# Weight matrices of a hybrid decoder step on one core: each load's bytes stored as one block, a partition's part in one piece

## What is computed

```python
h = rmsnorm(x, norm1_w)
proj = h @ w_in                       # 2048 x 8208: 8 gdn heads (q k v z), 16 gate columns, 8 hgrn heads (q f i z)
...                                   # causal conv, gated delta rule, HGRN2, gated head norms
x = x + mix @ w_out                   # 2048 x 2048
u = relu(rmsnorm(x, norm2_w) @ w_up)  # 2048 x 8192
x = x + (u * u) @ w_down              # 8192 x 2048
y = rmsnorm(x, final_norm_w)
```

## Time and profile before

| what | before |
|---|---|
| median of 3 runs (lowest, highest) | 2914.0 us (2912.57, 2924.3) |
| the profiled execution | 2909.2 us |
| its span, first to last instruction | 2907.5 us |
| TensorE, matmuls | 2869.8 us busy, 99% of the span |
| VectorE, ScalarE, GpSimd | 2056.6, 1137.7, 314.4 us busy |
| mean granted TensorE clock | 0.996 of full speed |
| traffic | 396.61 MB in 516,481 packets, mean 136 GB/s |

### The profile page before, as it was taken

How to read it: one execution, slowest core, us unless ns; L and a number is a source line. 1 busy time by engine, 2 the same in 40 slices (tenths; PEclk the granted TensorE clock), 3 DMA queues, 4 the chain that set the end, 5 groups by cost and what they waited for, 6 DMA issues and landing times.

```text
span 2907.5 us, 53032 instructions
## 1 busy us (share of the span) xinstructions
PE 2869.8 (99%) x22264; PEld 2802.5 (96%) x22264; DVE 2056.6 (71%) x2921; ACT 1137.7 (39%) x1432; POOL 314.4 (11%) x464
## 2 busy tenths in 40 slices
PE   9999999999999999999999999999999999999998
PEld 8999999899999999999999999999999999999998
DVE  6666666656575757665687777777778878888885
ACT  4333333333333333333444444444434444444454
POOL 6201111110101010102100000000000000000111
PEclk9999999999999999999999999999999999999999
DMA  7343647643434344444345544554586666666665
GB/s 211 70 92 73 93 72 79 81 93 74 86 79 87 80 79 80 122 130 139 90 140 156 157 136 146 154 154 136 151 255 205 193 204 192 188 193 203 191 193 199
DMA packets 516481, 396.61 MB, mean 136 GB/s; under 512 B 18930, under 2 KB 484196, under 8 KB 516244
## 3 DMA queue, kind: packets, MB, share of 16 engines
q1 hardware_dynamic: 462272, 267.95, 39.8%
q0 software_dynamic: 22672, 88.35, 8.3%
q10 hardware_dynamic: 31300, 36.93, 4.0%
HBM read 308.80 MB, written 84.37 MB: 135 GB/s over the span
## 4 chain that ended last, share of the span: by engine, by line
PE 84%; DVE 8%; ACT 3%; issue 2%; DMA 1%; ACTq 0%; DVEq 0%; POOL 0%; POOLq 0%
PE main L1369 40%; PE main L1003 26%; PE mx L1369 7%; PE mx L1252 2%; DVE w_lo L1969 1%; PE mx L1075 1%; PE mx L1151 1%; PE mx L1162 1%; PE main L1352 1%; DMA tmp<-rows_scratch 1%; DVE tmp L2090 1%; PE mx L1134 1%; PE mx L1091 1%; DMA mix_scratch<-tmp 1%; PE mx L1259 0%
## 5 line engine op out<-in xcount | busy, mean ns | idle before, releaser
L1369 PE MATMUL main<-forms_a,w_hi 128*128 128x288 f32 x3024 | 606.1, 296 | 4.4 <-DVE w_lo L2572 4.2
L1003 PE MATMUL main<-h_hi,w_hi 128*128 128x296 f32 (+1 forms) x2592 | 604.5, 314 | 4.7 <-DVE h_lo L1981 2.2
L1369 PE MATMUL main<-forms_b,w_hi 128*128 128x288 f32 x3024 | 603.8, 295 | 0.5 <-DVE w_lo L2572 0.5
L1003 PE MATMUL main<-h_lo,w_hi 128*128 128x296 f32 (+1 forms) x2592 | 563.4, 299 | 0.0
L1003 PE MATMUL main<-h_hi,w_lo 128*128 128x296 f32 (+1 forms) x2592 | 562.9, 298 | 0.0
L1369 PEld LDWEIGHTS main<-forms_a,w_hi 128*128 128x128 f32 x3024 | 487.1, 189 | 6.5 <-DVE w_lo L2572 6.5
L1369 PEld LDWEIGHTS main<-forms_b,w_hi 128*128 128x128 f32 x3024 | 484.5, 188 | 0.7 <-DVE w_lo L2572 0.7
L1369 PE MATMUL main<-forms_a,w_lo 128*128 128x288 f32 x1512 | 448.0, 296 | 0.0
L1369 PE MATMUL main<-forms_b,w_lo 128*128 128x288 f32 x1512 | 445.1, 294 | 0.0
L1003 PEld LDWEIGHTS main<-h_hi,w_hi 128*128 128x128 f32 x2592 | 413.0, 190 | 26.3 <-issue 13.3
L1003 PEld LDWEIGHTS main<-h_hi,w_lo 128*128 128x128 f32 x2592 | 420.9, 189 | 0.0
(11 more groups left out here) (404 smaller groups left out, 3467.3 us busy)
## 6 DMA issues: line engine op xcount, KB each, us to landing
w_raw<-in_w_in SPq DMA_DIRECT2D x128, 512.0 KB, 8.5
w_raw<-in_w_up SPq DMA_DIRECT2D x128, 512.0 KB, 5.6
w_raw<-in_w_down SPq DMA_DIRECT2D x100, 512.0 KB, 5.9
u_forms<-ub POOLq DMA_DIRECT2D x32, 1152.0 KB, 6.2
z<-x_scratch SPq DMA_DIRECT2D x32, 576.0 KB, 5.7
x_scratch<-z POOLq DMA_DIRECT2D x31, 576.0 KB, 5.8
stage<-u_forms ACTq DMA_DIRECT2D x30, 576.0 KB, 3.9
w_raw<-in_w_out SPq DMA_DIRECT2D x32, 512.0 KB, 4.0
```

Source lines behind the costliest of these rows:

```text
L1003: ins = mm(out[:, half, :], w[:, ring, k, :], x[:, kx, half * width:half * width + width], start=first and n == 0, stop=last_ and n == 2)
L1369: ins = mm(out, w[:, k, :], x[:, kx, :], start=i in (0, 1, 3) and k == 0 and n == 0, stop=k == KP - 1 and n == 2, skip_group_check=True)
```

## The change

The host hands over each of the four matrices in another order of its elements. Each 512 KB load then reads one block in which partition after partition has its 4 KB. The 16 gate columns of `w_in` become an input of their own, `w_gates`, of shape (2, 128, 8, 16), with 512 bytes for each partition. `w_down` is stored as (column tile, row tile parity, partition, row tile pair, 128): a partition has 16 KB in a row for 32 pairs, and a load takes 8 pairs of them, or n and 8 - n where the window wraps. The loads keep their number, their size, their order, their waits and their destinations. Nothing is changed on any other engine. The reordering is done before the launch.

```diff
-        w_in = io["w_in"][0].rearrange("(k p) n -> p k n", p=P)
-        w_out = io["w_out"][0].rearrange("(k p) n -> p k n", p=P)
-        w_up = io["w_up"][0].rearrange("(k p) n -> p k n", p=P)
-        w_down = io["w_down"][0].rearrange("(k p) n -> p k n", p=P)
+        w_gates, w_in, w_out, w_up, w_down = (io[n] for n in ("w_gates", "w_in", "w_out", "w_up", "w_down"))
...
-                sp.dma_start(w_raw[:, j, :, 0:2 * HEADS], w_in[:, UK * j:UK * j + UK, 4 * GK:4 * GK + 2 * HEADS]).then_inc(s_w[j], 16)
+                sp.dma_start(w_raw[:, j, :, 0:2 * HEADS], w_gates[j]).then_inc(s_w[j], 16)
...
-                    j = unit_order(h, i)
-                    col = (0 if j < 8 else HG0) + (j % 8) // 2 * GK
-                    k0 = UK * (j % 2)
-                    src = (w_in[:, k0:k0 + UK, col + h * P:col + h * P + P] if isinstance(h, int)
-                           else w_in[:, k0:k0 + UK, bass.ds(h * P + col, P)])
-                    load(src, h * 16 + (2 + i), (2 + i) % RAW)
+                    load(w_in[h, unit_order(h, i)], h * 16 + (2 + i), (2 + i) % RAW)
...
-                load(w_out[:, k0:k0 + UK, m * P:m * P + P], OUT_U0 + v, (OUT_U0 + v) % RAW)
+                load(w_out[m, k0 // UK], OUT_U0 + v, (OUT_U0 + v) % RAW)
...
-                    src = w_up[:, j % 2:KT:2, (2 * p + j // 2) * P:(2 * p + j // 2) * P + P]
+                    src = w_up[2 * p + j // 2, j % 2]
...
-                        src = w_down[:, 2 * q + j % 2:2 * (q + n_ - 1) + j % 2 + 1:2, m * P:m * P + P]
+                        src = w_down[m, j % 2, :, q:q + n_, :]
...
+def blocks(w, order):
+    return w.reshape(-1, P, w.shape[1] // P, P).transpose(2, 0, 1, 3).reshape((w.shape[1] // P,) + order + (P, P))
+
+def laid_out(inputs):
+    a = {name: inputs[name] for name in _INS}
+    w = a["w_in"][0]
+    tiles = w[:, 0:4 * GK], w[:, HG0:]
+    a["w_gates"] = w[:, 4 * GK:HG0].reshape(2, UK, P, 2 * HEADS).transpose(0, 2, 1, 3)
+    a["w_in"] = stacked([t.reshape(2, UK, P, 4, HEADS, P).transpose(4, 3, 0, 2, 1, 5) for t in tiles])
+    a["w_out"] = blocks(a["w_out"][0], (2, UK)).transpose(0, 1, 3, 2, 4)
+    for name in ("w_up", "w_down"):
+        a[name] = blocks(a[name][0], (a[name].shape[1] // P // 2, 2)).transpose(0, 2, 3, 1, 4)
+    return a
```

More of the change, by code:

```diff
@@ L2747, with stacked @@
         "final_norm_w"]
+def blocks(w, order):
[10 more added lines that the diff above has]
+    return a
+def stacked(parts):
+    import numpy as _np
+    return _np.concatenate(parts, axis=1).reshape(HEADS, 16, P, UK, P)
 _OUTS = [("y_prompt", (1, NP_, D)), ("y_sample", (SB, ST, D)), ("conv_prompt", (1, 1, PRE, 3 * GK)),
@@ L2760 @@
     arrays, io = {}, {}
-    for name in _INS:
-        a = _np.ascontiguousarray(inputs[name])
+    for name, a in laid_out({name: _np.asarray(inputs[name]) for name in _INS}).items():
+        a = _np.ascontiguousarray(a)
         arrays[f"in_{name}"] = a
```

## The result

The changed kernel takes **2898.2 us**, the median of 5 runs (2895.85 to 2899.36), against 2914.0 us of 5 runs of the kernel before on the same chip (2911.89 to 2924.3). Run once more beside other kernels, it took 2897.04 us (6 runs, 2892.86 to 2899.82) against 2914.44 (11 runs), 0.9943 [0.9928, 0.9958]. Its profiled execution took 2899.11 us, with a span of 2897.4 us and a granted clock of 0.997.

What follows compares the result with a forecast made beforehand. TensorE was taken to bound the kernel, at work for 2869.8 of 2907.5 us. Passage and start, 1.1 + 1.1 = 2.2 us off the profiled 2909.2, gave 2907.0, moved by 4.8 to 2911.8, say 2912 us; range 2903 to 2918.

Steps and rivals of the forecast that it cites:

- But for `w_in` nobody waits: Loads of `w_in`: expected to gain most, landing in 8.5 us against 4.0 for `w_out`, but no engine waits for them.
- Heads, output projection ...: nothing: Term for heads, output projection, `w_up` and later steps of `w_down`: no gain, as TensorE's own work covers the loads.
- arithmetic that no load enters: TensorE's waits on VectorE inside the heads, 4.5 us, once in each of 8 heads: no load was said to matter.
- The passage to `w_down`, 1.1 us: Near 2186 us, a late block delays ScalarE, VectorE and TensorE: quicker loads were to gain 1.1 us there.
- five blocks: In the passage to `w_down`, blocks counted among seven forms; 5 x (2.26 - 1.43) = 4.1 us as upper bound of the gain.
- The start, 1.1 us: Two gate loads become 128 pieces of 512 bytes instead of 1024 of 64, so VectorE starts sooner: 1.1 us, at most 2.2.
- Nothing moves: Rival, whole kernel: passage bound by bytes, start by VectorE, so the time stays 2914 us; chance 0.20, uncut pieces included.
- the slower one: Rival, `w_down` stage: 16 engines reading neighbouring addresses slow the loads, 68 us more, 2982 us; chance 0.04.
- the cut pieces: Rival, queue q1: pieces are cut again to 512 bytes, packets stay above 400,000, 2914 us; within the 0.20 for no movement.
- The large version: Rival, passage and start: 4.7 us of waits, 1.7 of clock and 2.2 at the start, 8.6 us, 2905 us; chance 0.11.
- Faster by more than can be missed: Rival, matmuls everywhere: their pace depends on the traffic, 1 ns each would be 22 us, 2892 us; chance 0.05.
- The rule of the Trainium skill that I had made a rival: Rival, all loads: 512 bytes suffice for full rate, so only the gates' 64-byte pieces gain, 2913 us; chance 0.20.

Runs made afterwards that it cites:

- Experiment 8: Kernel before, with heads 2 and 3 alone loading `w_in` from a padded copy (rows of 33,280 bytes): 2906.2 us, before 2916.57.
- experiment 10: Kernel before, with 64 columns of zeros behind the gate columns of `w_in` (rows of 33,088 bytes): 2900.36 us, before 2916.57.
- experiment 5: Kernel before, with `w_in` in blocks of 4 KB pieces, each 4160 bytes from the next: 2903.83 us, before 2914.42.
- Experiment 9: Kernel before, with all heads but 2 and 3 loading `w_in` from a padded copy (rows of 33,280 bytes): 2915.24 us, ratio 0.9998.

## Why the prediction was wrong

**"But for `w_in` nobody waits", and with it "Heads, output projection ...: nothing".** This is the step that failed. The observation is true: no engine waits for `w_in` in either trace. The conclusion is not. I costed the loads by who waits for them, and left out what they do to other transfers on the same 16 engines. A median of 8.5 us beside 4.0 for `w_out` was the sign. I cited it, and didn't ask in which stretch those 8.5 us arise or who else moves data there. Opened by heads, 8.5 is itself a mixture, with 19.0 us in head 3. What I had put at nothing comes to 10.1 us in the profiled pair. In six kernels that mend `w_in` alone the median lies 10.3 to 16.2 us under before's.

**The waits inside the heads as "arithmetic that no load enters".** Right for L1134, which is 4.5 us in all 8 heads and is still there. But under it stood smaller waits that come once. Those at L1237 and L1075 end on VectorE and ScalarE, which in their turn had waited for a DMA. I read the list from its top and stopped; the chain of waits, opened between 440 and 600 us, names the two transfers outright.

**The scatter.** The three runs of before, 2912.57 to 2924.3 us, I used for the width of the range. That scatter was probably a part of the effect. The kernels with the slow stretch scatter by 10 to 16 us (11 to 23 runs each), with standard deviations of 3.0 to 4.8 us. Those with quick loads of `w_in` throughout scatter by 1 to 8 us, though in 5 or 6 runs each, with standard deviations of 0.5 to 3.2. Experiment 8, whose stretch is gone, still scatters by 10.6 us, so the stretch is not all of it. The profiled execution, at 2909.2, was a mild case: its heads take 1323.1 us, those of the four other traces with the stretch 1329.6 to 1335.9. To move the forecast with it by 4.8 us was sound only if the same term is in all runs.

**The passage to `w_down`, 1.1 us.** The mechanism is right and the size too small. In the profiled pair TensorE's waits and the clock between 2140 and 2220 us come to 4.4 + 1.7 = 6.1 us before and 2.7 + 1.7 = 4.4 after, a gain of 1.7; that it is so near the 1.1 is luck of this pair. Over all traces the stage gives 726.7 - 721.7 = 5.0 us, which is near the upper bound that I had written, 4.7 + 1.7. I had taken it down because of a ceiling of 16 x 22.9 = 366 GB/s, and that ceiling was wrong: the changed kernel moves 398 and 403 GB/s here. The share of packet time in these stretches is 1.07 and 1.06, over 1, so packet times overlap, and a pace worked out from them over the whole span is no ceiling. Nor was the passage bound by the blocks' bytes alone: of what moves in it, between 2160 and 2180 us before, 60% are q1's pieces of the forms, 1152 bytes each, and 25% the 512-byte pieces of the blocks. After the change 50% and, now in 4 KB pieces, 26%. Only that quarter changed its pieces, and the rate of the whole rose by 15%: it is 392 to 403 GB/s in four traces with `w_down` in blocks, and 335 to 351 in four with it row by row. The "five blocks" of the upper bound don't come out of the code either, which puts three between the first form and the last and one behind; the sum didn't use them. The profiled execution of the changed kernel still has two waits:

```profile
PE main L1361 <- DVE w_lo L2564: 3.2, 3, 2.0
PE mx L1024 <- DMA x_tok<-in_x_prompt: 2.8, 1, 2.8
```

The 5.86 us of ScalarE's wait for the block are gone. Its `w_hi` at 2172.31 us now starts straight behind a form that had been waited for. What is late next is the form, and VectorE's backlog behind it, as the prediction had it:

```profile
2171.48 0.93 ACT L1862 ACTIVATE forms_a<-forms_a 128x864 fp32r<-128x864 f32 x1 [14.82 <-DMA forms_a<-u_forms]
2172.31 1.04 ACT L1797 ACTIVATE w_hi<-w_raw 128x1024 fp32r<-128x1024 f32 x1
...
2180.51 0.53 PE L1361 MATMUL main<-forms_a,w_hi 128*128 128x288 f32 x2 [0.74 <-DVE w_lo L2564]
```

**The start, 1.1 us.** Wrong in both halves. The pieces were not what I had priced (64 bytes stayed), and where they are really whole, the start is not measurably shorter. TensorE's wait for x, the second line above, is 2.8 us in one trace of the changed kernel and 2.3 in another: while the gates' loads are the same.

**Right.** The later steps of `w_down`: between 2220 and 2840 us TensorE is idle for 0.0 us in both traces, as the slack of 3.7 us said. The pace of the matmuls, 756 and 755. q1's share, 28% forecast and 28.4% measured, and its packets, 88,000 and 93,120: of the difference, 2048 - 256 = 1792 are the gates' and 28 x 128 = 3584 those of the 28 blocks of `w_down` that come in two parts, which I had put together. `w_in` under 5 us.

**The rivals.** "Nothing moves" and the slower one fell, and so did the cut pieces. The large version had the passage nearly right and gave 2905. "Faster by more than can be missed" had the direction with the wrong cause. The rule of the Trainium skill that I had made a rival ("DMA: Bandwidth & Descriptors", section "Specifications": 512 bytes suffice for full rate) is nearly borne out in the heads. Pieces of 512 bytes land in 4.0 us there once the rows lie well, against 3.5 for 4 KB, and nobody waits for the difference. In the passage it falls short: 344 and 351 GB/s against 398 and 403, with a quarter of the bytes in pieces of 512 bytes or of 4 KB. The other section of that page of the Trainium skill, "How a descriptor splits into AXI transactions", seemed to agree with the 8.5 us; experiment 10, with three rows in four off the boundary as before, shows that the boundary is not their cause, and experiment 5 agrees.

**What stays open.** Why the distance of 32,832 bytes is slow, and why in head 3 above all. That the stretch begins with head 3's first load and ends with its last, while the other heads run the same steps, speaks for the addresses of its columns; but no run loads these columns at another moment, so it is not shown. A longer row also moves every row and whatever lies behind the matrix in DRAM, which no run separates from the distance. Experiment 9 speaks against that second reason, for it has a further matrix in DRAM and the stretch is as it was.

Then the last line of the chain of experiment 9: an idle time of TensorE near 590 us that no semaphore ends. It is 1.0, 2.5, 3.95 and 6.9 us long in four of the five traces with the slow stretch, and in none of the 13 others. A late fetch of instructions would look so, and the packets of queue q8, kind "instruction" and 16 KB each, speak for it. In each of the four traces one of them ends 1.3 to 1.5 us before TensorE goes on (in that of experiment 9 at 591.62 us, and TensorE goes on at 593.11), 14 to 23 us after the one before it began, where 8 to 10 us lie between two such packets at that place in the traces without the stretch. Whose instructions they are the trace doesn't say, so this too is argued and not shown.

## What to carry to other kernels

A load that nobody waits for can still set the time, if it makes the transfers of others late that share the DMA engines with it. So read each load's landing by stretches (here by heads) rather than as one median, and where it stands out against loads of the same size, open the chain of waits in that stretch. Before laying a matrix out anew, try another distance between its rows: here one edit of 64 columns gave most of what the blocks gave.

Where runs of one kernel scatter more than those of its neighbours, look for a transfer that is at the edge of what its cover hides. Here that was a hint and no proof.

## What was not expected of the hardware

- The same 1024 pieces of 512 bytes take 8.5 us (median) at a row distance of 32,832 bytes, 19 us in head 3 and 6.0 to 9.4 in the others; at 33,024, 33,088 and 33,280 bytes they take 3.9 to 4.1 us in every head. The bytes and packets are the same; q1's share falls from 39.8 to between 32.7 and 33.2%.
- While these loads were slow, so were all other kinds of transfer between 400 and 560 us: 512 KB of state 23.1 against 6.0 us, 296 KB of mixed rows 14.6 against 2.5. ScalarE's queue needed 4.07 us to issue two loads, against 0.81.
- The stretch moved 76 GB/s in that time, where the changed kernel moved 79 and the passage 344, so the number of bytes is not what held the transfers up. The median packet of 512 bytes took 27 ns in and out of the stretch; the slowness is in a minority of packets.
- In the passage, where a quarter of the bytes are the blocks', 4 KB pieces for them raise the rate of the whole from 344 and 351 to 398 and 403 GB/s.
